# x in eight pieces between the first weight chunks, and the constants behind the fifth

## The reference, cut to what matters

```python
q_lat, kv_lat, k_pe, qd, kd, vd = jnp.split(h @ w_in, splits, axis=-1)   # h is x, 256 x 2048
q = (_rmsnorm(q_lat, q_norm) @ w_q_b)...
ple = (p[i] @ ple_w[i]) * jax.nn.sigmoid(h @ ple_gate_w[i])              # p[0] is needed much later
```

## Time and profile before

| what | us |
|---|---|
| median of 3 executions | 2518.15 (2512.46 to 2522.08) |
| the profiled execution: span from first to last instruction | 2516.6 |
| PE busy | 2348.2 (93%) |
| DVE busy | 1463.7 (58%) |
| ACT busy | 1031.9 (41%) |
| POOL busy | 632.5 (25%) |
| DMA | 483.02 MB, mean 192 GB/s |

### The profile page before, as it was taken

How to read it: one execution, slowest core, us unless ns; L and a number is a source line. 1 busy time by engine, 2 the same in 40 slices (tenths; PEclk the granted TensorE clock), 3 DMA queues, 4 the chain that set the end, 5 groups by cost and what they waited for, 6 DMA issues and landing times.

```text
span 2516.6 us, 32804 instructions
## 1 busy us (share of the span) xinstructions
PE 2348.2 (93%) x10996; PEld 1931.5 (77%) x10996; DVE 1463.7 (58%) x1714; ACT 1031.9 (41%) x1134; POOL 632.5 (25%) x537
## 2 busy tenths in 40 slices
PE   8999898999999889999768399989999999999996
PEld 6888687888788678888655388868888888888885
DVE  5544757657667685755663945565544454444455
ACT  4443534444444333444235044444444443444432
POOL 0000048329976687702730000010000000000001
PEclk9998999999999999999888699999999999999998
DMA  6554264678976658655585245646555555555553
GB/s 234 185 175 135 75 211 149 203 246 280 302 250 208 208 176 284 232 191 185 186 224 160 77 151 194 193 153 207 192 190 187 190 191 193 193 188 187 191 192 111
DMA packets 136992, 483.02 MB, mean 192 GB/s; under 512 B 18656, under 2 KB 19168, under 8 KB 135744
## 3 DMA queue, kind: packets, MB, share of 16 engines
q1 hardware_dynamic: 121568, 429.44, 52.3%
q0 software_dynamic: 14048, 50.80, 6.6%
q10 hardware_dynamic: 1280, 1.48, 0.2%
HBM read 457.80 MB, written 19.14 MB: 190 GB/s over the span
## 4 chain that ended last, share of the span: by engine, by line
PE 76%; POOL 7%; DMA 7%; DVE 6%; issue 2%; ACT 1%; DVEq 0%; SPq 0%; ACTq 0%; POOLq 0%
PE ps L351 24%; PE ps L353 24%; PE ps L352 24%; POOL s_c_pow L1501 3%; DMA raw<-in_w_inA 3%; POOL s_c_tmp L1501 1%; DVE w_lo L977 1%; PE ps L592 1%; PE ps L631 1%; DMA s_bt_raw<-in_s_bt 1%; PE ps L367 1%; POOL s_bt L1501 1%; DMA s_c_dram<-s_c_pow 1%; ACT w_hi L692 1%; POOL s_bt_tmp L1501 1%
## 5 line engine op out<-in xcount | busy, mean ns | idle before, releaser
L977 DVE TENSOR_TENSOR w_lo<-raw,w_hi 128x1024 fp32r<-128x1024 f32 (+1 forms) x782 | 1101.1, 1416 | 897.8 <-ACT w_hi L692 891.3
L692 ACT ACTIVATE w_hi<-raw 128x1024 fp32r<-128x1024 f32 (+1 forms) x782 | 821.6, 1053 | 1225.3 <-PE ps L353 1093.0
L351 PE MATMUL ps<-w_hi,x_hi 128*128 128x512 f32 (+1 forms) x2336 | 918.0, 393 | 19.6 <-DVE x_lo L985 14.5
L353 PE MATMUL ps<-w_hi,x_lo 128*128 128x512 f32 (+1 forms) x2336 | 911.1, 390 | 0.0
L352 PE MATMUL ps<-w_lo,x_hi 128*128 128x512 f32 (+1 forms) x2336 | 910.9, 390 | 0.0
L351 PEld LDWEIGHTS ps<-w_hi,x_hi 128*128 128x128 f32 x2336 | 443.4, 190 | 111.7 <-DVE x_lo L985 16.4
L353 PEld LDWEIGHTS ps<-w_hi,x_lo 128*128 128x128 f32 x2336 | 443.2, 190 | 91.4
L352 PEld LDWEIGHTS ps<-w_lo,x_hi 128*128 128x128 f32 x2336 | 443.7, 190 | 88.7
L351 PE MATMUL ps<-w_hi,hid_hi 128*128 128x512 f32 x704 | 277.1, 394 | 1.0 <-DVE w_lo L977 0.8
L1485 POOL TENSOR_TENSOR res<-res,gb 128x512 f32<-128x512 f32 x9 | 13.9, 1547 | 1044.4 <-ACT res L817 1044.4
L352 PE MATMUL ps<-w_lo,hid_hi 128*128 128x512 f32 x704 | 275.3, 391 | 0.0
(11 more groups left out here) (192 smaller groups left out, 1491.3 us busy)
## 6 DMA issues: line engine op xcount, KB each, us to landing
raw<-in_w_inA SPq DMA_DIRECT2D x192, 512.0 KB, 4.3
raw<-in_w_inB SPq DMA_DIRECT2D x160, 512.0 KB, 4.0
raw<-in_w_outA SPq DMA_DIRECT2D x96, 512.0 KB, 3.8
raw<-in_w_outB SPq DMA_DIRECT2D x80, 512.0 KB, 4.3
raw<-in_w_in SPq DMA_DIRECT2D x64, 512.0 KB, 3.8
raw<-in_w_gate SPq DMA_DIRECT2D x64, 512.0 KB, 4.3
raw<-in_w_glu SPq DMA_DIRECT2D x64, 512.0 KB, 4.3
raw<-in_w_out SPq DMA_DIRECT2D x32, 512.0 KB, 4.3
```

The lines of the kernel that those rows point to most:

```text
L351: pe.matmul(o, hi[:, kt + k, cols], WH[:, s, k, 0:width], start=(kt + k == 0), stop=False)
L353: last = pe.matmul(o, lo[:, kt + k, cols], WH[:, s, k, 0:width], start=False, stop=(kt + k == depth - 1))
L692: act.activation(WH[:, s, :, 0:width], RAW[:, s, :, 0:width], ACT.Copy).then_inc(hi_ready, 1)
L977: dve.tensor_tensor(WL[:, s, :, 0:width], RAW[:, s, :, 0:width], WH[:, s, :, 0:width].bitcast(F32), ALU.subtract).then_inc(lo_ready, 1)
```

## The change

SP loads x in eight pieces of 256 columns: piece 0, chunk 0, piece 1, chunk 1, piece 2, chunk 2, piece 3, chunk 3, piece 4, and then pieces 5 to 7. ACT issues only the identity at the start; the seven others follow in `constants()`, behind the high part of chunk 4, p first. PE turns group 0, and then each group j+1 behind chunk j. p is turned behind chunk 8 and split behind chunk 9, and the angles are computed behind the low part of chunk 10.

```diff
-        x_in = [sem(f"x_in{n}") for n in range(4)]
+        x_in = [sem(f"x_in{n}") for n in range(8)]
...
-            def load_x(q4):
-                cols = slice(WB * q4, WB * (q4 + 1))
-                sp.dma_start(RES[:, :, cols], xv[:, :, cols]).then_inc(x_in[q4], 16)
+            def load_x(g):
+                cols = slice(256 * g, 256 * (g + 1))
+                sp.dma_start(RES[:, :, cols], xv[:, :, cols]).then_inc(x_in[g], 16)
 
             load_x(0)
-            load_x(1)
...
                     for j in range(first):
                         load(w, j, j, 0, None, width)
-                        if j < 2:
-                            load_x(2 + j)
+                        load_x(1 + j)
+                    for g in range(first + 1, 8):
+                        load_x(g)
...
             def turn_x(g):
-                if g % 2 == 0:
-                    pe.wait_ge(x_in[g // 2], 16)
+                pe.wait_ge(x_in[g], 16)
                 turn(TG["x"] + g, RES[:], 256 * g)
 
             turn_x(0)
-            turn_x(1)
...
                     if b == 0:
-                        if j < 6:
-                            turn_x(j + 2)
-                        elif j == 6:
-                            pe.wait_ge(p_in, 16)
-                            turn(TG["p0"], PK[:], 0)
                         pe.wait_ge(turned, TG["x"] + j + 1)
                     chunk(c0 + per * b + j, 0, None, XH, XL, 2 * j, KT, (b0 + b) % 2)
+                    if b == 0 and j < 7:
+                        turn_x(j + 1)
+                    if b == 1 and j == 0:
+                        pe.wait_ge(p_in, 16)
+                        turn(TG["p0"], PK[:], 0)
...
+            def constants():
+
+                act.dma_start(PK[:], t["p"][0].rearrange("(t p) n -> p t n", p=P)).then_inc(p_in, 16)
+                for dst, name in [(CM[:], "causal"), (PI[:], "pos")]:
+                    act.dma_start(dst, t[name]).then_inc(const_in, 16)
+                act.dma_start(B0[:], t["dil_bias"][:, 0:2]).then_inc(const_in, 16)
+                act.dma_start(NG[:], t["norm_gain"].partition_broadcast(P)).then_inc(const_in, 16)
+                for q in range(TT):
+                    act.dma_start(AT[:, 3, q, :], t["inv_freq"].partition_broadcast(P)).then_inc(const_in, 16)
...
                     hi(8 * b + j)
-                    if b == 0 and j == 7:
+                    if b == 0 and j == 4:
+                        constants()
+                    if b == 1 and j == 1:
                         hi_turned(TG["p0"], PH[:])
...
                     lo(8 * b + j)
-                    if b == 0 and j == 7:
+                    if b == 1 and j == 1:
                         lo_turned(TG["p0"], HG["p0"], PH[:], PLO[:])
-                    if j == 0 and b == 1:
+                    if j == 2 and b == 1:
                         angles()
```

More of the change, by code:

```diff
@@ L677, in _ @@
             act.dma_start(ID[:], t["ident"]).then_inc(ident_in, 16)
[L678 to L684, removed]
             def hi(c, coef=0, i=None, width=WB):
```

## The result

The changed kernel takes 2555.86 us (median of 4, 2549.22 to 2558.88) against 2520.11 (median of 4, 2512.46 to 2525.87): ratio 1.0135, 95% interval 1.0117 to 1.0153, so 29 to 39 us slower. The profiled execution has a span of 2554.1, 37.5 over the one before. The forecast was 2550, with 2538 to 2561 as its range.

The account below looks back on a forecast made before the run. The start was taken as bound by transfers up to 21.86, then by PE. Terms of +0.5, +18.0 and +4.1 (22.6) plus 9.6 for the clock gave 32.2 on 2516.6, so 2550 for a median, range 2538 to 2561.

Parts of the forecast that it names:

- chunk 0 starts: Start of block 0: smaller loads let chunk 0 start at 8.8 (7.2 to 11.75), 2.46 us earlier than 11.75.
- chunk 1 starts, against before: First gap: chunk 0, transposes and the chain put chunk 1 at 17.7 against 17.17, +0.5 us (bounds -1.5 and +3.5).
- a gap, a period at the upper clock: Block 0: after each group's transposes PE idles 2.95 us for ACT and DVE; chunk, transposes and gap take 6.39 us.
- chunks 1 to 7 without the clock: Block 0: six periods of 6.39 us take 38.3 us where before it took 20.3, so +18.0 us.
- the clock, all eight gaps: PE's clock falls behind three of four of eight gaps, 1.6 us each: +9.6 us (bounds 0 and 25).
- chunks 7 to 12: Later p and angles delay the low parts and normalization before chunk 12: +4.1 us (bounds 0 and +6).
- wait before the normalized block: Before chunk 12: PE stands idle 3.4 us for the normalized block, against 0.91 before the change.
- The bound: Before: start bound by transfers up to 21.86, then by PE without gaps; a 2.95 us chain was hidden, groups two ahead.
- The transfers: Start: x's first piece lands at about 4.3, chunk 0's load at 6.3 (bounds 4.7 and 9.29).
- The constants: ACT's seven issues, 3.8 us between chunk 4's high part and group 5's copy, are hidden with 1.1 to spare: cost 0.
- the clock stays up: Rival: same gaps in block 0 but the clock never falls, 2541 us; chance 0.14.
- The rival of the other side: Block 0 gaps don't open (under 0.7 us), earlier transfers count fully: -4.4 us, 2514; hidden or half hidden gaps 0.05.

Follow-up runs that it names:

- weights_first: The changed kernel, but in block 0 ACT and DVE split chunk j before group j, PE's order unchanged: 2532.85 us, ratio 1.0056.
- pieces_alone: The kernel before with only the eight alternating pieces of x; constants, PE's order, p and angles as before: 2520.02 us, ratio 1.0002.
- the fills: The changed kernel with 5, 8 or 10 extra unused matmuls behind each turned group in block 0: 2545.16, 2538.54, 2536.26 us.
- order_alone: The kernel before, its pieces and constants untouched, with the changed kernel's PE order and places of p and angles: 2557.87 us, ratio 1.0149.

## Why the prediction was right

| step | forecast | measured |
|---|---|---|
| chunk 0 starts | 8.8 | 8.53 |
| chunk 1 starts, against before | 17.7, +0.5 | 17.01, -0.2 |
| a gap, a period at the upper clock | 2.95, 6.39 | 2.98, 6.40 |
| chunks 1 to 7 without the clock | +18.0 | 6 x 6.40 - 20.3 = +18.1 |
| the clock up to chunk 7 | in the 9.6 | 47.0 - 38.4 = +8.6 |
| the clock, all eight gaps | +9.6 | 8.6 + 1.7 + 1.2 = +11.5 |
| chunks 7 to 12 | +4.1 | +6.0, of which 1.7 is the clock in chunk 7 |
| wait before the normalized block | 3.4 | 3.13 |
| shift at chunk 12, at chunk 13 | 32.2 | 85.53 - 53.03 = 32.5, 89.58 - 55.88 = 33.7 |
| whole span | 32.2 | 37.5; by the ratio 29 to 39 |

The bound. Before, PE's stream was closed from chunk 2 on the earlier trace rows, and the change opened it in seven places. That the same chain stood in the old trace, hidden behind a chunk, gave the gap before it existed; weights_first, which takes two of its three instructions on ACT and DVE out, confirms it. The last 0.11 of the 2.95 was luck: it ran from the low part's end at 28.14 to 28.25, the start of a chunk that didn't wait for it. The real hand-over took 0.14 (31.00 to 31.14).

The transfers. Chunk 0's load was issued at 1.27 in the changed kernel, and this is its time to landing:

```profile
DMA to landing us min/median/max: 4.7/4.7/4.7
```

So it landed at 6.0, against the 6.3 of the forecast. ACT began its high part at 6.07, when the copy of group 0 was done, so two things ended within 0.1 us there: the weights, and the chain behind x's first piece, which PE began to turn at 4.46. The forecast priced only the first of them (it had 4.3 for the piece); had the weights landed earlier, chunk 0 would have started no earlier than it did. The gain at chunk 0 is real, 3.2 us, and of it chunk 1 has 0.2 left; the forecast had it 0.5 late. No run shows that smaller pieces cost time as a whole, which the forecast allowed for: pieces_alone has ratio 1.0002 (0.9992 to 1.0013).

The constants. Forecast at 3.8 us of ACT with 1.1 to spare; they took 3.3, from 34.68 to 38.00, begun while the copies before them still ran, and ACT's next work came at 43.89. The cost is 0.

The clock. Forecast from four gaps of other stages: three in four fall. The old trace has two more that it didn't list (each gap, and the stretch behind it with columns as in the earlier trace rows):

```profile
268.76 0.57 PE L458 MATMUL ps<-ident,probs 128*128 128x128 f32 x3 [2.01 <-DVE probs L1150]
268.80:275.90 7.10, 6.33 (x24) 5.25 (x25) 6.17 (x22) 3.57 (x15) 0.00 (x0) 0.52 0.00 0
1669.74 0.80 PE L351 MATMUL ps<-w_hi,x_hi 128*128 128x512 f32 x1 [4.50 <-DVE x_lo L985]
1669.80:1675.40 5.60, 5.60 (x13) 4.45 (x14) 5.57 (x4) 0.07 (x1) 5.44 (x5) 0.50 0.26 92
```

Behind both the clock was down, and for longer than the 3.3 us that the forecast took for a fall. In the changed kernel six of the eight gaps had a fall behind them, just the three in four. Two periods were at the full 6.40, the other four longer by 1.3 to 2.9, chunk 7 by 1.7 and chunk 12 by 1.2: 11.5 in all, 1.9 for each fall instead of 1.6. So the share was right and the cost of one was taken a little too low. Of the 10.3 up to chunk 12 the fills took 9 back. The rival "the clock stays up" is refuted by its own number: 2541 against 2549 and more, and by the granted clock of 0.67 from 40 to 60. The Trainium skill, "TensorE: Matmul & The Clock Gate", section "HAM oscillation — how this bites in real kernels", describes this very pattern, bursts that begin at the lower clock after each wait; the trace agrees in part, for of the bursts of chunks 1 to 7 three began at the lower clock (1, 4 and 6), two fell to it within 0.5 us of their start (5 and 7), and two kept the upper one. Where the forecast read it strictly, so that gaps this short would pass, the runs disagree: behind gaps of 2.98 the clock fell in most periods, and behind gaps of 1.41 in none.

What was too small is the remainder: the forecast had all as before behind chunk 12. At chunk 13 the shift is 33.7, and 3.8 more come by the end, spread over the span. Most of this can be the scatter of one profile: nine other kernels gain up to 2.3 or lose up to 3.5 there (see the fills). order_alone, with the same order as the changed kernel, is 39.6 late at chunk 13 and 40.1 at the end.

The rival of the other side needed gaps under 0.7; they were 2.98. But its gain was real: with the order restored, and p and the angles too, the same loads are 2 to 7 us faster than before, near the 4.4 that it priced.

## What to carry to other kernels

When a producer is moved next to its consumer in an in-order program, look up in the trace how long its chain through the other engines is and what covers it now: here 2.95 us were covered by running two groups ahead, and the place of one line cost 30 us, some seven times the 4.5 that the earlier transfers could give. Price a recurring gap of PE twice, once as idle time and once for the clock that it may cost behind it. Judge the parts of a combined change apart: late constants (-2.6 us at chunk 5), small pieces (nothing alone), p and the angles (+4.6 up to chunk 12), the order (+30).

## What the runs showed that was not expected

- Useless matmuls in the gaps made the kernel 18 us faster (1.0135 to 1.0063); 9 of them are seen in the profile up to chunk 12. The rest is more than the scatter of the other profiles behind it and isn't explained.
- Gaps of 1.82 behind bursts of a chunk, a group and five matmuls brought one fall of the clock in seven; gaps of 2.98 brought it down in most, gaps of 1.41 never (in the changed kernel and order_alone, three of twelve periods were at 6.4).
- ACT issued transfers (34.68) while its own earlier copies were still running, so seven issues cost nothing in the changed kernel; in weights_first, where ACT has less to spare, the gap behind them is 0.3 longer (1.72 against 1.41).
